# Partial sums of squared residual tiles on GpSimd at three layer ends of a four-layer decoder trunk

## The reference

```python
def rms_norm(x, g):
    y = xf * lax.rsqrt(jnp.mean(xf * xf, axis=-1, keepdims=True) + EPS)
    return y * g

for layer in range(DEPTH):
    h = rms_norm(x, g[0]); y = mixer(h)
    x = x + rms_norm(y, g[1])
    h = rms_norm(x, g[2]); y = memory_cross_attn(h, mem_k[layer], mem_v[layer], w_q, w_o)
    x = x + rms_norm(y, g[3])
```

## Time and profile before

| | us |
|---|---|
| median of 3 runs | 2017.1 |
| lowest and highest run | 2013.8, 2017.39 |
| span of the profiled execution | 2015.7 |
| TensorE busy (share of the span) | 1951.5 (97%) |
| VectorE busy | 1244.4 (62%) |
| ScalarE busy | 930.6 (46%) |
| GpSimd busy | 1008.8 (50%) |
| mean granted clock of TensorE | 0.986 |

### The profile page before, as it was taken

One profiled execution on the slowest core, in us unless ns is written; L12 is line 12 of the kernel. 1 busy time (PEld: TensorE's weight loads), 2 busy tenths in 40 slices (PEclk: granted clock), 3 DMA queues, 4 the chain that ended last, 5 costly groups with the idle time before them and its releaser, 6 DMA issues.

```text
span 2015.7 us, 35615 instructions
## 1 busy us (share of the span) xinstructions
PE 1951.5 (97%) x13890; PEld 1763.9 (88%) x13890; DVE 1244.4 (62%) x2220; ACT 930.6 (46%) x1557; POOL 1008.8 (50%) x1249
## 2 busy tenths in 40 slices
PE   7999999999999999999999999999999999999997
PEld 5998989798888988897889999999998889989976
DVE  5988342426887787755147777777454157874552
ACT  3676522334555555342354444443243347674333
POOL 4776704026555655250356666566631337776602
PEclk8999999999999999999999999999999999999998
DMA  4444476535444544487353444444586344445870
GB/s 130 149 147 135 135 250 231 208 105 174 124 116 132 151 132 140 138 297 241 113 170 108 130 130 130 137 136 146 165 313 211 132 148 141 135 148 166 292 231 27
DMA packets 332615, 324.64 MB, mean 161 GB/s; under 512 B 19768, under 2 KB 313056, under 8 KB 332448
## 3 DMA queue, kind: packets, MB, share of 16 engines
q1 hardware_dynamic: 330944, 321.49, 49.8%
q10 hardware_dynamic: 1504, 0.87, 0.2%
HBM read 292.16 MB, written 29.61 MB: 160 GB/s over the span
## 4 chain that ended last, share of the span: by engine, by line
PE 75%; DVE 14%; ACT 5%; issue 2%; DMA 2%; POOL 1%; SPq 1%; DVEq 0%; ACTq 0%
PE ps L773 10%; PE ps L774 10%; PE ps L778 10%; PE ps L1458 5%; PE ps L1467 4%; PE ps L1261 3%; PE ps L1524 2%; PE ps L888 2%; PE ps L763 2%; PE ps L765 2%; PE ps L764 2%; ACT wh L1713 2%; DVE work L2543 2%; PE ps L1602 1%; PE ps L1541 1%
## 5 line engine op out<-in xcount | busy, mean ns | idle before, releaser
L1693 POOL TENSOR_TENSOR wl<-raw,wh 128x256 fp32r<-128x256 f32 x1216 | 1003.3, 860 | 979.1 <-ACT wh L1713 978.9
L1713 ACT ACTIVATE wh<-raw 128x1024 fp32r<-128x1024 f32 x304 | 311.8, 1053 | 202.1 <-PE ps L778 49.8
L773 PE MATMUL ps<-Hh,wh 128*128 128x320 f32 x1200 | 372.2, 324 | 2.8 <-DVE work L2563 0.9
L774 PE MATMUL ps<-Hl,wh 128*128 128x320 f32 x1200 | 360.4, 314 | 0.0
L773 PEld LDWEIGHTS ps<-Hh,wh 128*128 128x128 f32 x1200 | 230.0, 192 | 11.3 <-DVE work L2427 2.3
L774 PEld LDWEIGHTS ps<-Hl,wh 128*128 128x128 f32 x1200 | 230.4, 192 | 2.1
L2258 DVE TENSOR_SCALAR work<-ps 128x512 f32<-128x512 f32 (+8 forms) x220 | 100.3, 474 | 170.9 <-PE ps L871 39.8
L778 PE MATMUL ps<-Hh,wl 128*128 128x320 f32 x1200 | 201.1, 310 | 0.0
L778 PEld LDWEIGHTS ps<-Hh,wl 128*128 128x128 f32 x1200 | 183.2, 189 | 0.1
L773 PE MATMUL ps<-Oh,wh 128*128 128x320 f32 x512 | 152.2, 310 | 3.7 <-DVE Ol L3004 3.7
L774 PE MATMUL ps<-Ol,wh 128*128 128x320 f32 x512 | 151.1, 308 | 0.0
(11 more groups left out here) (439 smaller groups left out, 3922.0 us busy)
## 6 DMA issues: line engine op xcount, KB each, us to landing
raw<-rg_w_in SPq DMA_DIRECT2D x128, 256.0 KB, 3.5
raw<-hg_w_in SPq DMA_DIRECT2D x128, 256.0 KB, 4.8
raw<-ssd_w_in SPq DMA_DIRECT2D x96, 256.0 KB, 3.9
work<-cache_mem_k SPq DMA_DIRECT2D x40, 512.0 KB, 6.3
work<-cache_mem_v SPq DMA_DIRECT2D x40, 512.0 KB, 5.1
raw<-rg_w_out SPq DMA_DIRECT2D x64, 256.0 KB, 3.6
raw<-x_w_k SPq DMA_DIRECT2D x64, 256.0 KB, 3.6
raw<-x_w_v SPq DMA_DIRECT2D x64, 256.0 KB, 3.7
```

The costliest lines, as they stand in the source:

```text
L773: pe.matmul(ps[:, bank, 0:n], high(half, k), mh[:, k, 0:n], start=(k == 0), stop=False)
L774: pe.matmul(ps[:, bank, 0:n], high(half, k), ml[:, k, 0:n], start=False, stop=False)
L1693: ins = pool.tensor_tensor(out, src, wh[:, parted(n) % HALVES, r:r + 2].bitcast(F32), ALU.subtract)
L1713: act.activation(wh[:, nx.n % HALVES], raw[:, slot, :, half * P:(half + 1) * P], ACT.Copy).then_inc(hi_ready, 1)
```

## The change

At the ends of layers 0, 1 and 2, GpSimd adds the squared tiles 1 to 4 to tile 0, one after the other, each as soon as ScalarE has squared it. TensorE sums tile 0 with the squared tiles 5, 6 and 7: four products with ones in place of eight. A new event sq_pooled, the third and later counts of the semaphore `consts`, tells TensorE that tile 0 is ready. In GpSimd's program the adds stand ahead of `low` for the first unit of the next mixer.

```diff
+        POOLED = 4
@@ TensorE
+            def sum_pooled(L, n, bank):
+
+                pe.wait_ge(*past("sq_pooled", L + 1))
+                pe.matmul(ps[:, bank, 0:NT], ones[:], SQ[:, 0], start=True, stop=False)
+                for k in range(POOLED + 1, KD):
                     pe.wait_ge(*past("sq_ready", n * KD + k + 1))
                     mm = pe.matmul(ps[:, bank, 0:NT], ones[:], SQ[:, k], start=False, stop=(k == KD - 1))
                 mm.then_inc(S("ssq_full"), 1)
@@ TensorE, attention(L)
-                sum_squares(5 + 4 * L, 7)
+                sum_pooled(L, 5 + 4 * L, 7)
@@ GpSimd
+            def add_squares(L):
+                n = 5 + 4 * L
+                for k in range(1, POOLED + 1):
+                    pool.wait_ge(*past("sq_ready", n * KD + k + 1))
+                    if k > 1:
+                        steps.sync()
+                    ins = pool.tensor_tensor(SQ[:, 0], SQ[:, 0], SQ[:, k], ALU.add)
+                    if k < POOLED:
+                        steps.did(ins)
+                    else:
+                        ins.then_inc(S("sq_pooled"), 1)
+
             for n in PARTED:
+                if n in MIX_AT[1:]:
+                    add_squares(MIX_AT.index(n) - 1)
                 low(n)
```

## The result

| | before | changed |
|---|---|---|
| median of the runs, us | 2017.2 (8 runs, 2009.0 to 2023.2) | 2005.1 (8 runs, 2000.9 to 2009.1) |
| span of the profiled execution, us | 2015.7 | 2002.0 |
| mean granted clock in it | 0.986 | 0.989 |

The ratio is 0.9947, with a 95% interval of 0.9929 to 0.9964. On 2016 us that is 10.7 us less, 7.3 to 14.3.

A forecast was written before the change was run, and what follows sets the result against it. TensorE, busy 97% of the span, was taken to bound the kernel. Three ends at 2.16 us each gave 6.5 us less, nothing charged for the adds: 2010.6 us for the median, range 2007.0 to 2015.5.

The forecast's parts named there:

- What bounds the kernel, what goes: TensorE bounds; at each of three layer ends four products of 0.54 us leave the critical chain, 2.16 us.
- The adds: Four GpSimd adds at a layer end, hidden: over at 442.9 us, 1.0 us before TensorE arrives.
- A step: One GpSimd add with its wait on its own result, beside VectorE's residual: 1.31 us.
- The residual: VectorE's residual at a layer end: each add delays one instruction by 0.67 us, 2.7 us in all, still covered.
- The cover of the fourth product: In the new sum, the last square is ready 0.5 us before TensorE's fourth product wants it.
- The first rival: Squared tiles come late at the layer ends and take part of the gain back: 2012.5 us, chance 0.15.
- The sum: Total over three layer ends: 3 x 2.16 = 6.5 us gained, nothing charged.
- The third rival: Gain made but given back elsewhere through falls of TensorE's clock: 2016.0 us; chance 0.11 together with the fourth rival.

The follow-up runs named there:

- e4: Against the kernel before: GpSimd's four adds at each of three ends go to a spare tile, TensorE still sums eight products; ratio 0.9997 (0.9983 to 1.0011).
- e16: The changed kernel with five adds on GpSimd and three products on TensorE at each end; ratio 0.9960 (0.9946 to 0.9975) to the kernel before.
- e17: The kernel before with one weight block loaded ahead of the state load in SyncE's queue in HGRN2; ratio 0.9965 (0.9950 to 0.9980), 7.1 us less.
- e18: The changed kernel with one weight block loaded ahead of the state load in SyncE's queue; ratio 0.9948 (0.9927 to 0.9969) to the kernel before, median 2006.4 us.

## Why the prediction was right in kind and wrong in size

**What bounds the kernel, what goes: right.** L800 (L802 in the changed kernel) went from 80 to 32 records. The sum takes 2.15 us instead of 4.31 at each end, and L789 waits the 0.53 us of before at the first.

**The adds: right.** A step was forecast at 1.31 us; an add took 0.92 to 1.01 us, and two with the wait between them 2.08. Against the forecast the four didn't run back to back: GpSimd waited 0.93 us for a square after the second. The two errors nearly cancel, so it is partly luck that the last add was over 1.16 us ahead of TensorE (forecast 1.0). e4 shows no cost of the adds within its interval, e16 that the cover ends with the fourth.

**The residual: right.** Forecast 2.7 us of delay for the last square. It is at 442.18 where before it was at 442.35, in a trace that stands 2.72 us earlier at this point, so the delay is 2.55 us. The cover of the fourth product was 0.66 us (forecast 0.5). The first rival, late tiles, didn't come about. The rule of the Trainium skill's page SBUF — State Buffer, section Who interferes with whom, that the two engines exclude each other, comes close here. The VectorE instruction started 0.13 to 0.21 us after the add, with some 0.8 us of the add to go, was held up 0.61 to 0.66 us, and ended 0.35 us after it, where it takes 0.48 to 0.55 us undisturbed. So it ran beside the add for at most 0.2 us. The forecast of four delays of 0.67 us was right, the first rival's of four whole adds, 3.7 us, too dear.

**The sum: the wrong step.** "3 x 2.16 = 6.5 us gained, nothing charged" took the stages there to move forward as blocks. They don't. HGRN2 has waits for weights that are late because SyncE's queue stands behind the landing of a store, and that term, put at nothing, measured 3.2 us: seven traces in which HGRN2 isn't moved wait 2.4 to 5.8 us (mean 4.2), nine in which it starts 2 to 4 us earlier wait 0.2 to 2.5 (mean 1.0). The row that should have warned me was in the list of waits: `L1261 <- POOL wl L1693: 4.6, 3, 2.1`. It is TensorE waiting on the path, in a stage that I took to move as a block. The third rival, a gain or loss elsewhere, was near to it but priced another thing, the falls of the clock, and mostly as a loss. Of those its sentence "both kernels are equally exposed" holds (8.1 and 7.9 falls in the mean of the two groups); of the waits it doesn't.

**What stays open.** Why moving HGRN2 ahead keeps the slow stores away isn't shown. A head start doesn't explain it, since a later start lessened the waits too (1.2 and 2.7 us), nor does the time in the trace at which the stage starts. At the third end 2.2 and 3.8 us of products gave 0.4 us more and 1.8 us less time, which may be the spread of the runs alone. In the traces with a changed third end, layer 3 from its first mixer product to its last transpose takes 367.7 to 368.7 us (seven traces, mean 368.0), without 364.2 to 369.5 (eleven with the same work in layer 3, mean 367.0), which would be one of the two us that are missing. The rest, and its cause, I don't know. That the parts don't add up was measured at the first and the second end. That the waits of HGRN2 carry most of what is beyond the products is shown by the traces and by e17 and e18 within their intervals; e17's gain of 7.1 us is larger than the 4.6 us of waits that it takes away, and where the rest comes from isn't shown.

## What to carry to other kernels

A piece of the critical path that goes is worth its duration only if the stages behind it move as a block; look through them for waits on a transfer whose issue stands in a queue behind another transfer's landing, and let such a wait widen the range to both sides. Such a queue is worth mending for itself: one line moved in SyncE's order gave the kernel before 7.1 us, about as much as the products of the whole change are worth. And to price one edit, time it in parts and once near the very end of the kernel, where hardly anything can shift. Make the parts larger than the interval of a run: here parts of 2.2 us stood against 3 us to either side, and several of them say nothing alone.

## What the runs showed of the hardware

- GpSimd adds two float32 tiles of 128x320 in 0.92 to 1.00 us, all of these beside VectorE (L1713, and L1714 in e4); with two tiles of 128x256 the subtraction of L1693 took 0.74.
- VectorE's two-input instructions of 0.49 and 0.55 us take 1.15 us when they start 0.13 to 0.21 us after an add of GpSimd, and end 0.35 us after it.
- The same store of a state, eight times in HGRN2, landed after 3.2 us or after 5.1 us (3 of 8 over 5 us in the trace of before, none in that of the changed kernel), with nothing in between but a few of 3.7 and 4.7.
- Executions of one and the same kernel spread over 14 us (2008.9 to 2023.3, 23 runs of before made together), and over all runs the time goes down by some 1.2 us for each 0.001 of mean granted clock.
- A wait of TensorE of 2.07 us had a fall of the clock right behind it, worth 1.7 us, where a wait of 0.46 us at the same product had none. Over all traces, each of the 13 such waits of 1.7 us or more (of L1261, or L1272) has a fall within 1.2 us behind its end, and no shorter one has; but the falls of HGRN2 are no more in number for it (12 in e18, which has no such wait).
